# Three experts' items of at most 64 tokens, with high and low parts side by side

## The chip, the cores and the metric

One core of one Trainium2 chip runs the whole program. The metric is the device time of one execution in microseconds, from runs of the kernel before and the changed one. Engine names: TensorE (PE in rows, PEld its weight loads), VectorE (DVE), ScalarE (ACT), GpSimd (POOL), SyncE (SP), which issues most of the DMAs.

## What is computed

Two layers of a hybrid mixer on 256 tokens of 1024 values in float32. Layer 0 ends in a dense feed-forward stage, layer 1 in a mixture of experts, which is what the change is about:

```python
D_MODEL, N_EXPERTS, TOP_K, D_FF_EXPERT = 1024, 8, 2, 3584
logits = (ht @ w_router) + b_router
top_v, top_i = lax.top_k(logits, TOP_K)
probs = jax.nn.softmax(top_v, axis=-1)
gates = jnp.sum(jax.nn.one_hot(top_i, N_EXPERTS) * probs[..., None], axis=1)
for e in range(N_EXPERTS):
    a = jax.nn.silu(ht @ w_gate[e]) * (ht @ w_up[e])
    out = out + gates[:, e:e + 1] * (a @ w_down[e])
```

The 256 tokens make 512 choices of an expert. From the reference and its inputs, experts 0 to 7 get 54, 82, 58, 66, 52, 72, 42 and 86 of them.

## The kernel before

Every product is made of split operands: a float32 value is written as a high part (`whi`, `hhi`, `ahi`, rounded to `F32R`) and a low part, the rest. `mm3` (lines 763 to 766) then does three matmuls: high by high, low by high, high by low. In the expert stage the weights are the moving operand of 512 columns and the tokens, up to 128, the stationary one.

The expert stage works in items. An item is up to `CAP` = 128 tokens of one expert; items 0 to 7 are the experts in the order 0 to 7, and an expert with more than 128 tokens gets another item behind them (up to `ITEMS` = 11). Item 0 is written out by hand, items 1 to `last` - 1 run in a loop whose bound is a register read from `eid`, the last is written out again. An item has `E_CHUNKS` = 7 chunks of 512 hidden columns. A chunk takes six weight loads of 1 MB, slots s: two for gate, two for up, two for down.

The way of a slot: SP (`load`, line 477, called by `load_round`) fetches it into one of six ring places in `z` once VectorE has finished with the slot six before it. ScalarE writes its high part into a lane of `whi` (`e_hi_of`, line 418) once TensorE has used the lane's former slot, VectorE writes the low part (`e_lo_of`, line 424), and TensorE uses both. There are three or four lanes by the table `E_LANES`. The order on each engine is written by hand in `e_round`, `item` and `edge`:

- TensorE: `e_gate` into bank 0, `e_turn` of the former chunk's activations (four turns, line 773), `e_up` into bank 1, two `e_down` into banks 3 and 4, 24 matmuls each for gate, up and down. Near an item's end `turn_gathered` turns the next item's tokens.
- ScalarE: per chunk six casts of weights, the high part of the activations (`e_hi`, line 1628) and silu (line 1624). At an edge also the high part of the next tokens (`gathered_hi`, line 1617) and the item's output into `ysb` (`y_out`).
- VectorE: per chunk six subtractions of weights, the product silu by up (`e_mult`, line 2266) and the activations' low part (`e_lo`, line 1735). At an edge the low part of the next tokens (`e_lo_tokens`, line 1736).
- GpSimd: per item it gathers the next item's tokens from `tok_rows` by indirect DMA (line 736) and stores the item's rows to `out_rows` (line 738). At the end it gathers from `out_rows` the rows that each token needs, and VectorE adds them up with the gates' weights.

Routing: VectorE finds the two experts of each token, the places within each expert (`posx`) and, from the counts, `big`, `rank` and the table `eid` of each item's expert (lines 2244 to 2260), and sets `route_ok`. SP waits for it ahead of item 1's loads, and the other engines ahead of item 1. GpSimd waits for it too, works out each choice's row (lines 687 to 708), makes the late picks (line 711) that TensorE turns in item 0 (`turn_picks`), and writes and reads a table of tokens by item (lines 720 and 722).

## Time and profile before

| what | value |
|---|---|
| runs | 1728.37, 1728.77, 1729.31 us, median 1728.77 |
| profiled execution, span from its first to its last instruction | 1726.9 us |
| TensorE, VectorE, ScalarE, GpSimd busy | 1718.0, 1382.8, 1102.2, 111.9 us |
| bytes moved by DMA | 498.41 MB |

For the profiled execution the profile gives the span alone; what lies around the span is 1.9 us by the runs' median. Busy times are unions of an engine's instructions. Matmuls are pipelined, so one of 0.39 us starts every 0.23 us in a stream. A DMA share is the mean busy share of 16 DMA engines, and goes a little over 1 in short stretches. The expert stage begins at about 772 us and ends with the program.

### The profile page before, as it was taken

The numbers are of one execution on the slowest core, as the hardware profiler recorded it, in microseconds if no ns is written. First come the engines' busy times: TensorE is split into PE (matmuls) and PEld (weight loads), VectorE is DVE, ScalarE is ACT, GpSimd is POOL, SyncE is SP. The second block draws the span as 40 slices with busy tenths as digits, with TensorE's granted clock in tenths as the row PEclk, the third lists the DMA queues.
The fourth block names the chain that finished last, engine by engine and source line by source line (L and its number), as shares of the span: only waits on it lengthen the run. The fifth ranks groups of instructions, "written<-read, shape, count | busy, mean of one in ns | idle before, by whom it ended". The sixth has DMA issues, their size and how long they took to land.

```text
span 1726.9 us, 22649 instructions
## 1 busy us (share of the span) xinstructions
PE 1718.0 (99%) x8320; PEld 1435.9 (83%) x8320; DVE 1382.8 (80%) x1154; ACT 1102.2 (64%) x980; POOL 111.9 (6%) x114
## 2 busy tenths in 40 slices
PE   9999999999999999999999999999999999999998
PEld 8888888888888888888888888888888888888887
DVE  7875588555578755889889889889888898898898
ACT  4446564444344466557777777777777777777775
POOL 0021000000000200017000000000000000000100
PEclk9999999999999999999999999999999999999999
DMA  8653366553455424659999999999999999999994
GB/s 293 233 205 117 122 229 234 195 189 127 171 171 200 171 86 147 219 220 338 411 362 412 373 370 409 369 367 399 344 411 385 353 411 372 367 411 365 376 413 198
DMA packets 219848, 498.41 MB, mean 289 GB/s; under 512 B 8296, under 2 KB 13168, under 8 KB 219632
## 3 DMA queue, kind: packets, MB, share of 16 engines
q1 hardware_dynamic: 216096, 483.44, 75.6%
q0 software_dynamic: 3696, 14.18, 2.2%
q8 instruction: 40, 0.66, 0.1%
q14 instruction: 16, 0.13, 0.0%
HBM read 491.80 MB, written 7.88 MB: 289 GB/s over the span
## 4 chain that ended last, share of the span: by engine, by line
PE 96%; ACT 1%; DVE 1%; DMA 0%; issue 0%; POOL 0%; SPq 0%; DVEq 0%; POOLq 0%
PE ps L764 30%; PE ps L766 30%; PE ps L765 30%; PE ps L773 4%; PE ps L769 3%; ACT sb_w L1448 0%; DVE sb_wlo L395 0%; DMA sb_ringa<-in_w_in_dram 0%; ACT sb_whi L380 0%; DVE sb_w L1722 0%; ACT sb_ahi L1505 0%; DVE sb_z L1832 0%; ACT L1448 0%; DVE sb_wlo L424 0%; ACT sb_z L1498 0%
## 5 line engine op out<-in xcount | busy, mean ns | idle before, releaser
L424 DVE TENSOR_TENSOR sb_wlo<-sb_z,sb_whi 128x2048 fp32r<-128x2048 f32 x334 | 756.4, 2289 | 95.5 <-ACT sb_whi L418 94.8
L418 ACT ACTIVATE sb_whi<-sb_z 128x2048 fp32r<-128x2048 f32 x333 | 634.7, 1927 | 168.8 <-PE ps L766 164.9
L764 PE MATMUL ps<-sb_whi,sb_hhi 128*128 128x512 f32 (+2 forms) x1752 | 684.1, 390 | 0.0
L766 PE MATMUL ps<-sb_wlo,sb_hhi 128*128 128x512 f32 (+2 forms) x1752 | 676.0, 386 | 0.0
L765 PE MATMUL ps<-sb_whi,sb_hlo 128*128 128x512 f32 (+2 forms) x1752 | 675.7, 386 | 0.0
L766 PEld LDWEIGHTS ps<-sb_wlo,sb_hhi 128*128 128x128 f32 x1752 | 329.0, 188 | 66.8
L764 PEld LDWEIGHTS ps<-sb_whi,sb_hhi 128*128 128x128 f32 x1752 | 329.3, 188 | 65.3 <-issue 2.2
L765 PEld LDWEIGHTS ps<-sb_whi,sb_hlo 128*128 128x128 f32 x1752 | 329.4, 188 | 63.1
L764 PE MATMUL ps<-sb_whi,sb_ahi 128*128 128x512 f32 x560 | 219.1, 391 | 0.0
L766 PE MATMUL ps<-sb_wlo,sb_ahi 128*128 128x512 f32 x560 | 218.0, 389 | 0.0
L765 PE MATMUL ps<-sb_whi,sb_alo 128*128 128x512 f32 x560 | 218.0, 389 | 0.0
L395 DVE TENSOR_TENSOR sb_wlo<-sb_z,sb_whi 128x2048 fp32r<-128x2048 f32 (+1 forms) x70 | 153.3, 2197 | 75.0 <-ACT sb_whi L380 74.9
L380 ACT ACTIVATE sb_whi<-sb_z 128x2048 fp32r<-128x2048 f32 (+1 forms) x71 | 131.2, 1850 | 119.6 <-PE ps L766 118.5
L380 ACT ACTIVATE sb_whi<-sb_ringa 128x2048 fp32r<-128x2048 f32 x52 | 99.7, 1917 | 88.7 <-PE ps L766 76.8
L395 DVE TENSOR_TENSOR sb_wlo<-sb_ringa,sb_whi 128x2048 fp32r<-128x2048 f32 x52 | 118.6, 2286 | 31.2 <-ACT sb_whi L380 31.1
L766 PEld LDWEIGHTS ps<-sb_wlo,sb_ahi 128*128 128x128 f32 x560 | 105.1, 188 | 22.0
L765 PEld LDWEIGHTS ps<-sb_whi,sb_alo 128*128 128x128 f32 x560 | 105.2, 188 | 21.4
L764 PEld LDWEIGHTS ps<-sb_whi,sb_ahi 128*128 128x128 f32 x560 | 105.2, 188 | 21.4
L1628 ACT ACTIVATE sb_ahi<-ps 128x512 fp32r<-128x512 f32 x56 | 33.7, 602 | 42.7 <-PE ps L773 42.7
L773 PE MATMUL ps<-sb_const,sb_z 128*128 128x128 f32 x422 | 59.0, 272 | 0.5 <-DVE sb_z L2266 0.5
L773 PEld LDWEIGHTS ps<-sb_const,sb_z 128*128 128x128 f32 x422 | 50.5, 140 | 10.6 <-DVE sb_z L2266 0.9
L1735 DVE TENSOR_TENSOR sb_alo<-ps,sb_ahi 128x512 fp32r<-128x512 f32 x66 | 44.8, 685 | 14.6 <-ACT sb_ahi L1573 10.5
(274 smaller groups left out, 966.0 us busy)
## 6 DMA issues: line engine op xcount, KB each, us to landing
sb_z<-in_moe_w_gate_dram SPq DMA_DIRECT2D x112, 1024.0 KB, 6.9
sb_z<-in_moe_w_up_dram SPq DMA_DIRECT2D x112, 1024.0 KB, 6.8
sb_z<-in_moe_w_down_dram SPq DMA_DIRECT2D x112, 1024.0 KB, 7.1
sb_ringa<-in_w_in_dram SPq DMA_DIRECT2D x43, 1024.0 KB, 5.0
sb_z<-in_w_in_dram SPq DMA_DIRECT2D x24, 1024.0 KB, 5.0
sb_z<-in_ffn_w_up_dram SPq DMA_DIRECT2D x10, 1024.0 KB, 12.5
sb_z<-in_ffn_w_gate_dram SPq DMA_DIRECT2D x10, 1024.0 KB, 5.1
sb_z<-in_ffn_w_down_dram SPq DMA_DIRECT2D x10, 1024.0 KB, 5.0
```

What stands on the lines that cost most here:

```text
L380: nc.scalar.activation(whi[:, k, 0:n], raw[:, 0:n], ACT.Copy).then_inc(hi_done, 1)
L395: nc.vector.tensor_tensor(wlo[:, k, 0:n], raw[:, 0:n], whi[:, k, 0:n].bitcast(F32), ALU.subtract).then_inc(split, 1)
L418: nc.scalar.activation(e_lane(s)[0], ringb[:, s % RING_B, :], ACT.Copy).then_inc(hi_done, 1)
L424: nc.vector.tensor_tensor(lo, ringb[:, s % RING_B, :], hi.bitcast(F32), ALU.subtract).then_inc(split, 1)
L764: nc.tensor.matmul(out, lh, rh, start=start, stop=False)
L765: nc.tensor.matmul(out, ll, rh, start=False, stop=False)
L766: return nc.tensor.matmul(out, lh, rl, start=False, stop=stop)
L769: return nc.tensor.matmul(out, l, r, start=start, stop=stop)
L773: return nc.tensor.transpose(out, src, ident[0:n, 0:n])
L1628: nc.scalar.activation(ahi[:, :, at:at + CAP], ps[:, 2, :].rearrange("p (k c) -> p k c", k=4), ACT.Copy).then_inc(a_hi, 1)
L1735: return V.tensor_tensor(out, src, hi.bitcast(F32), ALU.subtract)
```

## The change

The seven experts 1 to 7 are ordered by their count of tokens (`fewer`, `order`), and that is the order of items 1 to 7. The first `FEW` = 3 of them hold up to `HC` = 64 tokens, the others 128; more tokens go to further items behind. In a small item the 64 tokens' high and low parts stand side by side as stationary columns (`hhi` holds high, high, low, high). Up and down take two matmuls instead of three, (high, low) by the weights' high part and by their low part, so that rows 0 to 63 and 64 to 127 of the result hold two summands. Gate must be whole in both halves, since silu comes next, and keeps three (`twice`). The turn multiplies by a constant of 64 columns that adds the halves, the activations then get their high and low part side by side in `ahi`, and for down the halves are added by the stores: GpSimd stores all 128 rows, waits, and stores rows 64 to 127 onto the first 64 with an adding DMA (`store_sum`). VectorE keeps four small operations of the routing; the rest goes to GpSimd, and `route_ok` is set by it after the table's stores. SP's program stays as it is.

```diff
+FEW = 3
+HC = P // 2
...
+            pool.wait_ge(rank_ok, 1)
+            link(pool.tensor_scalar(runs[:, 1:], order, FEW - 0.5, None, ALU.is_gt))
+            pool.tensor_scalar(room[:, 1:], runs[:, 1:], float(CAP - HC), float(HC), ALU.mult, ALU.add)
+            link(pool.tensor_scalar(first_of[:, 1:], order, 1.0, None, ALU.add))
+            link(pool.tensor_tensor(big, cnt, room, ALU.subtract))
+            link(pool.tensor_scalar(big, big, 0.5, None, ALU.is_gt))
+            link(pool.tensor_tensor(sums[:, 1, NE:], big, sums[:, 0, NE - 1:2 * NE - 1], ALU.add))
+            link(pool.tensor_tensor(sums[:, 2, NE:], sums[:, 1, NE:], sums[:, 1, NE - 2:2 * NE - 2], ALU.add))
+            link(pool.tensor_tensor(rank, sums[:, 2, NE:], sums[:, 2, NE - 4:2 * NE - 4], ALU.add))
+            link(pool.tensor_scalar(rank, rank, float(NE - 1), None, ALU.add))
+            pool.tensor_tensor(pos, posx, per_token(room), ALU.subtract)
+            link(pool.tensor_tensor(selx, rank, first_of, ALU.subtract))
+            link(pool.tensor_scalar(pos, pos, -0.5, None, ALU.is_gt))
             link(pool.tensor_tensor(item_, pos, per_token(selx), ALU.mult))
...
+            link(pool.tensor_scalar(more_of, rank, 1.0, None, ALU.add))
+            link(pool.tensor_tensor(more_of, more_of, big, ALU.mult))
+            link(pool.tensor_scalar(more_of, more_of, 1.0, None, ALU.subtract))
+            link(pool.tensor_tensor(found, places_of.unsqueeze(1).to_broadcast([P, ITEMS, 2 * NE]),
+                                    iota[:, 0:ITEMS].unsqueeze(2).to_broadcast([P, ITEMS, 2 * NE]), ALU.subtract))
+            link(pool.tensor_scalar(found, found, 0.0, None, ALU.is_equal))
+            for c in range(2):
+                m = pool.tensor_tensor(found[:, :, c * NE:(c + 1) * NE], found[:, :, c * NE:(c + 1) * NE],
+                                       iota[:, 0:NE].unsqueeze(1).to_broadcast([P, ITEMS, NE]), ALU.mult)
+            link(m)
+            for n in (8, 4, 2):
+                link(pool.tensor_tensor(found[:, :, 0:n], found[:, :, 0:n], found[:, :, n:2 * n], ALU.add))
+            pool.tensor_copy(eidf[:, 14:15], rank[:, NE - 1:NE])
+            pool.tensor_scalar(eidf[:, 15:16], rank[:, NE - 1:NE], 1.0, None, ALU.add)
+            link(pool.tensor_tensor(eidf[:, 0:ITEMS].unsqueeze(2), found[:, :, 0:1], found[:, :, 1:2], ALU.add))
+            pool.tensor_copy(eid[:, :], eidf[0:1, :]).then_inc(route_ok, 1)
...
+            def fetch_next(j):
+
                 wait_then(gather_mm, j * 2 + 2)
                 pool.tensor_copy(idx_now, idx[:, bass.ds(j + 13, 1)]).then_inc(idx_ok, 1)
                 wait_then(idx_ok, j + 1)
                 pool.indirect_dma_start(tok, None, tok_rows, at_rows(idx_now)).then_inc(tok_in, 16)
                 wait_then(y_ok, j + 1)
+
+            def store(j):
+
+                fetch_next(j)
                 pool.dma_start(out_rows[bass.ds(j * P, P), :], ysb[:, :]).then_inc(rows_out, 16)
+
+            def store_sum(j, n):
+
+                fetch_next(j)
+                pool.dma_start(out_rows[bass.ds(j * P, P), :], ysb[:, :]).then_inc(rows_half, 16)
+                wait_then(rows_half, n * 16 + 16)
+                pool.dma_start(out_rows[bass.ds(j * P, HC), :], ysb[HC:P, :], accum_op=ALU.add).then_inc(rows_out, 16)
+
+            store(0)
+            with pool.Fori(0, FEW) as n:
+                store_sum(n + 1, n)
+            with pool.Fori(FEW + 1, last) as j:
+                store(j)
...
+                def twice(out, k, hi, lo, start, stop):
+
+                    mm(out, hhi[:, k, HC:HC + P], hi, start, False)
+                    mm(out, hhi[:, k, 2 * HC:2 * HC + P], hi, False, False)
+                    return mm(out, hhi[:, k, 0:P], lo, False, stop)
+
+                def pair_of(out, parts, hi, lo, start, stop):
+
+                    mm(out, parts, hi, start, False)
+                    return mm(out, parts, lo, False, stop)
...
+                            if not few:
+                                m = mm3(ps[:, bank, :], hhi[:, k, 0:CAP], hlo[:, k, 0:CAP], hi[:, kk, :], lo[:, kk, :],
+                                        k == 0, k == KD - 1)
+                            elif bank == 0:
+                                m = twice(ps[:, bank, :], k, hi[:, kk, :], lo[:, kk, :], k == 0, k == KD - 1)
+                            else:
+                                m = pair_of(ps[:, bank, :], hhi[:, k, HC:HC + P], hi[:, kk, :], lo[:, kk, :],
+                                            k == 0, k == KD - 1)
...
                     for k in range(4):
-                        m = turn(ps[:, 2, k * P:(k + 1) * P], act_sb[:, 0, k * P:(k + 1) * P])
+                        if few:
+                            m = mm(ps[:, 2, k * HC:(k + 1) * HC], act_sb[:, 0, k * P:(k + 1) * P], halves)
+                        else:
+                            m = turn(ps[:, 2, k * P:(k + 1) * P], act_sb[:, 0, k * P:(k + 1) * P])
                     m.then_inc(a_t, 1)
...
+                            if few:
+                                m = pair_of(ps[:, 3 + half, :], ahi[:, k, at:at + P], hi[:, kk, cols], lo[:, kk, cols],
+                                            first and k == 0, last and k == 3)
+                            else:
+                                m = mm3(ps[:, 3 + half, :], ahi[:, k, at:at + CAP], alo[:, k, at:at + CAP],
+                                        hi[:, kk, cols], lo[:, kk, cols], first and k == 0, last and k == 3)
...
-                with pe.Fori(1, last) as j:
+                with pe.Fori(1, FEW + 1) as j:
+                    item(j, few=True)
+                with pe.Fori(FEW + 1, last) as j:
                     item(j)
...
+                        src, dst = gathered(n, k), hhi[:, k, 0:CAP]
+                        if few:
+                            src = src[:, 0:HC].unsqueeze(1).to_broadcast([P, 4, HC])
+                            dst = hhi[:, k, :].rearrange("p (c n) -> p c n", n=HC)
+                        m = nc.scalar.activation(dst, src, ACT.Copy, scale=par("norm2", KD + k))
...
-                def e_hi(n, at=0):
+                def e_hi(n, at=0, few=False):
                     act.wait_ge(a_t, n + (F_TILES + 1))
-                    nc.scalar.activation(ahi[:, :, at:at + CAP], ps[:, 2, :].rearrange("p (k c) -> p k c", k=4),
+                    c = HC if few else CAP
+                    nc.scalar.activation(ahi[:, :, at:at + c], ps[:, 2, 0:4 * c].rearrange("p (k c) -> p k c", k=4),
                                          ACT.Copy).then_inc(a_hi, 1)
...
-                link(V.tensor_scalar(big, ps[:, 4, 0:NE], float(CAP), None, ALU.is_gt))
-                link(V.tensor_tensor_scan(rank, ones[:, 0:NE], big, 0.0, ALU.mult, ALU.add))
-                V.tensor_scalar(eidf[:, 14:15], rank[:, NE - 1:NE], float(NE - 1), None, ALU.add)
-                link(V.tensor_scalar(eidf[:, 15:16], rank[:, NE - 1:NE], float(NE), None, ALU.add))
-
...
-                for n in range(EXTRA):
-                    second(n)
-                    pick_sum(iota[:, 0:NE], eidf[:, NE + n:NE + n + 1])
-                V.tensor_copy(eid[:, :], eidf[0:1, :]).then_inc(route_ok, 1)
+                link(V.tensor_copy(cnt, ps[:, 4, 0:NE]))
+                link(V.scalar_tensor_tensor(out=key, in0=cnt, scalar=float(NE), in1=iota[:, 0:NE], op0=ALU.mult,
+                                            op1=ALU.add))
+                others = [P, NE - 1, NE - 1]
+                link(V.tensor_tensor(fewer, key[:, 1:].unsqueeze(1).to_broadcast(others),
+                                     key[:, 1:].unsqueeze(2).to_broadcast(others), ALU.is_lt))
+                V.tensor_reduce(order, fewer, AX, ALU.add).then_inc(rank_ok, 1)
...
+                    c = HC if few else CAP
+                    lo = ahi[:, :, at + HC:at + P] if few else alo[:, :, at:at + CAP]
+                    minus_hi(lo, ps[:, 2, 0:4 * c].rearrange("p (k c) -> p k c", k=4), None,
+                             ahi[:, :, at:at + c]).then_inc(a_lo, 1)
...
+                        c = HC if few else CAP
+                        lo = hhi[:, k, 2 * HC:3 * HC] if few else hlo[:, k, 0:CAP]
+                        m = minus_hi(lo, gathered(j, k)[:, 0:c], par("norm2", KD + k), hhi[:, k, 0:c])
...
-                with dve.Fori(1, last) as j:
-                    edge(j - 1)
+                edge(0, few_next=True)
+                with dve.Fori(1, FEW) as j:
+                    item(j, few=True)
+                    edge(j, few=True, few_next=True)
+                item(FEW, few=True)
+                edge(FEW, few=True)
+                with dve.Fori(FEW + 1, last) as j:
                     item(j)
-                edge(last - 1)
```

On TensorE, in the loop over an item's chunks, the second half of a gate product, the turn and the following products stood so (`sb_whi`, `sb_wlo` are the weights' parts, `sb_hhi`, `sb_hlo` the tokens', `sb_ahi`, `sb_alo` the activations'; `sb_const` in the turn is the identity):

```order
L764 MATMUL ps<-sb_whi,sb_hhi 128x512
L765 MATMUL ps<-sb_whi,sb_hlo 128x512
L766 MATMUL ps<-sb_wlo,sb_hhi 128x512
...
L773 MATMUL ps<-sb_const,sb_z 128x128 x4
L355 REGISTER_ALU
L764 MATMUL ps<-sb_whi,sb_hhi 128x512
L765 MATMUL ps<-sb_whi,sb_hlo 128x512
L766 MATMUL ps<-sb_wlo,sb_hhi 128x512
...
L764 MATMUL ps<-sb_whi,sb_ahi 128x512
L765 MATMUL ps<-sb_whi,sb_alo 128x512
L766 MATMUL ps<-sb_wlo,sb_ahi 128x512
```

In a small item's loop the same place now reads:

```order
L833 MATMUL ps<-sb_whi,sb_hhi 128x512 x2
L833 MATMUL ps<-sb_wlo,sb_hhi 128x512
...
L833 MATMUL ps<-sb_const,sb_z 128x64 x4
L370 REGISTER_ALU
L833 MATMUL ps<-sb_whi,sb_hhi 128x512
L833 MATMUL ps<-sb_wlo,sb_hhi 128x512
...
L833 MATMUL ps<-sb_whi,sb_ahi 128x512
L833 MATMUL ps<-sb_wlo,sb_ahi 128x512
```

Gate keeps three matmuls for each of its eight parts, up and down have two; the turn is four matmuls with 64 columns.

On GpSimd, from the wait for the routing to the last operation before a choice's row is picked out, stood (the names in square brackets are semaphores; `pool_chain` is the engine's wait for its own former result):

```order
L687 TENSOR_SCALAR sb_st<-sb_st 128x8 [waits route_ok]
L688 TENSOR_TENSOR sb_st<-sb_st,sb_const 128x8 [waits pool_chain]
L689 TENSOR_SCALAR sb_root<-sb_st 128x16 [waits pool_chain]
L690 TENSOR_TENSOR sb_st<-sb_root,sb_st 128x16 [waits pool_chain]
L691 TENSOR_TENSOR sb_st<-sb_st,sb_const 128x16 [waits pool_chain]
L692 TENSOR_SCALAR sb_root<-sb_root 128x16 [waits pool_chain]
L693 TENSOR_TENSOR sb_root<-sb_root,sb_st 128x16 [waits pool_chain]
L694 TENSOR_SCALAR sb_st<-sb_st 128x16 [waits pool_chain]
L695 TENSOR_TENSOR sb_st<-sb_st,sb_root 128x16 [waits pool_chain]
L696 TENSOR_SCALAR sb_root<-sb_root 128x16 [waits pool_chain]
L697 TENSOR_TENSOR sb_st<-sb_root,sb_st 128x16 [waits pool_chain]
```

Now the same stretch begins with

```order
L705 TENSOR_SCALAR sb_const<-sb_const 128x7 [waits rank_ok]
L706 TENSOR_SCALAR sb_const<-sb_const 128x7 [waits pool_chain]
L707 TENSOR_SCALAR sb_const<-sb_const 128x7
L708 TENSOR_TENSOR sb_const<-sb_st,sb_const 128x8 [waits pool_chain]
L709 TENSOR_SCALAR sb_const<-sb_const 128x8 [waits pool_chain]
L710 TENSOR_TENSOR sb_const<-sb_const 128x8 [waits pool_chain]
L711 TENSOR_TENSOR sb_const<-sb_const 128x8 [waits pool_chain]
L712 TENSOR_TENSOR sb_st<-sb_const 128x8 [waits pool_chain]
L713 TENSOR_SCALAR sb_st<-sb_st 128x8 [waits pool_chain]
L714 TENSOR_TENSOR sb_root<-sb_st,sb_const 128x16 [waits pool_chain]
L715 TENSOR_TENSOR sb_st<-sb_st,sb_const 128x8
L716 TENSOR_SCALAR sb_root<-sb_root 128x16 [waits pool_chain]
```

and eight more follow as before, 20 operations instead of 11, and it waits for `rank_ok` instead of `route_ok`. Behind the table's four stores and ahead of its reading stands a block of 14 operations that was not there:

```order
L752 TENSOR_TENSOR sb_const<-sb_const 128x176 [waits pool_chain]
L754 TENSOR_SCALAR sb_const<-sb_const 128x176 [waits pool_chain]
L756 TENSOR_TENSOR sb_const<-sb_const 128x11x8 [waits pool_chain]
...
L761 COPY sb_st<-sb_st 128x1 [waits pool_chain]
L762 TENSOR_SCALAR sb_st<-sb_st 128x1
L763 TENSOR_TENSOR sb_st<-sb_const 128x11
L764 CAST sb_eid<-sb_st 1x16 [waits pool_chain]
L767 DMA sb_idx<-table_dram 128x11 [waits table_out]
L772 TENSOR_LOAD sb_eid [waits rows_filled,route_ok,tok_stored,table_rows]
```

Its last one sets `route_ok`, for which SP, TensorE, ScalarE and VectorE wait before item 1.

## Rows read from the trace of the kernel before

**Rows 1.** The page's busy times: engine, busy us, share of the span, instructions.

```profile
PE 1718.0 (99%) x8320; PEld 1435.9 (83%) x8320; DVE 1382.8 (80%) x1154; ACT 1102.2 (64%) x980; POOL 111.9 (6%) x114
```

**Rows 2.** Timeline, GpSimd: start us, us, line, operation, count, idle before.

```profile
1011.92 0.57 POOL L738 DMA_DIRECT2D out_rows_dram<-sb_ysb  x1 [114.18 <-ACT sb_ysb L1635]
...
1130.35 0.57 POOL L738 DMA_DIRECT2D out_rows_dram<-sb_ysb  x1 [114.19 <-ACT sb_ysb L1635]
```

**Rows 3.** Windows, one period: PE, PEld, DVE, ACT, POOL busy, clock, DMA share, GB/s.

```profile
892.90:1011.30 118.40, 118.40 (x542) 98.19 (x541) 104.98 (x65) 89.54 (x66) 3.38 (x3) 1.00 1.01 381
```

**Rows 4.** Timeline, TensorE, a chunk of an item in the loop.

```profile
1093.36 0.60 PE L773 MATMUL ps<-sb_const,sb_z 128*128 128x128 f32 x4
...
1099.27 0.39 PE L764 MATMUL ps<-sb_whi,sb_ahi 128*128 128x512 f32 x1
...
1104.71 0.39 PE L764 MATMUL ps<-sb_whi,sb_hhi 128*128 128x512 f32 x1
...
1110.15 0.60 PE L773 MATMUL ps<-sb_const,sb_z 128*128 128x128 f32 x4
```

**Rows 5.** Waits from 900 to 1700 us: us in total, times, longest.

```profile
ACT sb_whi L418 <- PE ps L766: 142.9, 169, 3.5
DVE sb_wlo L424 <- ACT sb_whi L418: 82.3, 132, 1.6
...
ACT sb_whi L418 <- DMA sb_z<-in_moe_w_up_dram: 1.8, 3, 0.7
```

**Rows 6.** Timeline, VectorE, the same chunk and the edge behind it.

```profile
1096.91 4.49 DVE L424 TENSOR_TENSOR sb_wlo<-sb_z,sb_whi 128x2048 fp32r<-128x2048 f32 x2 [1.24 <-ACT sb_whi L418]
1101.33 0.68 DVE L2266 TENSOR_TENSOR sb_z<-sb_z,ps 128x512 f32<-128x512 f32 x1
1101.92 4.52 DVE L424 TENSOR_TENSOR sb_wlo<-sb_z,sb_whi 128x2048 fp32r<-128x2048 f32 x2
...
1119.18 2.15 DVE L1736 SCALAR_TENSOR_TENSOR sb_hlo<-ps,sb_small,sb_hhi 128x128 fp32r<-128x128 f32 x8
```

**Rows 7.** Timeline, ScalarE, the same chunk.

```profile
1094.96 3.73 ACT L418 ACTIVATE sb_whi<-sb_z 128x2048 fp32r<-128x2048 f32 x2
```

**Rows 8.** Windows, an item's edge, columns as in group 3.

```profile
1120.00:1125.00 5.00, 5.00 (x25) 4.15 (x24) 4.61 (x9) 5.00 (x4) 0.00 (x0) 1.00 0.71 270
```

**Rows 9.** DMA from 1140 to 1200 us, then 1620 to 1700: bytes, issues, us to landing.

```profile
DMA packets 10516, 24.67 MB, mean 411 GB/s; under 512 B 399, under 2 KB 399, under 8 KB 10516
...
sb_z<-in_moe_w_gate_dram SPq DMA_DIRECT2D x6, 1024.0 KB, 6.7
...
DMA packets 13366, 33.04 MB, mean 413 GB/s; under 512 B 526, under 2 KB 526, under 8 KB 13364
...
sb_z<-in_moe_w_gate_dram SPq DMA_DIRECT2D x8, 1024.0 KB, 10.2
```

**Rows 10.** Timeline, GpSimd, the routing.

```profile
770.94 0.27 POOL L687 TENSOR_SCALAR sb_st<-sb_st 128x8 f32<-128x8 f32 x1 [5.84 <-DVE sb_eid L2260]
...
774.18 2.24 POOL L697 TENSOR_TENSOR sb_st<-sb_root,sb_st 128x16 f32<-128x16 f32 x1
...
803.20 2.71 POOL L720 DMA_INDIRECT table_dram<-sb_idx  x1 [0.61 <-issue]
...
829.64 2.20 POOL L736 DMA_INDIRECT sb_w<-tok_rows_dram,sb_idx  x1 [0.84 <-POOL sb_idx L734]
```

**Rows 11.** Timeline, TensorE in item 0: turn of the picks, of item 1's tokens.

```profile
817.19 0.38 PE L773 MATMUL ps<-sb_const,sb_z 128*128 128x128 f32 x2
...
873.73 1.04 PE L773 MATMUL ps<-sb_const,sb_w 128*128 128x128 f32 x8
```

**Rows 12.** Timeline, SyncE's queue, item 1's first loads.

```profile
869.83 3.09 SPq L477 DMA_DIRECT2D sb_z<-in_moe_w_gate_dram  x2
```

**Rows 13.** DMA from 900 to 1700 us, the token gathers.

```profile
sb_w<-tok_rows_dram,sb_idx POOLq DMA_INDIRECT x5, 9.2
```

**Rows 14.** Windows, the start of the program, columns as in group 3.

```profile
5.00:10.00 5.00, 3.39 (x31) 3.20 (x29) 2.34 (x5) 3.12 (x7) 0.00 (x0) 1.00 0.97 327
```

More of the change, by code:

```diff
@@ L246, in build, with ranked @@
         tok = w1t[:, 0, :]
+        at_rank = CONST["mlmask"][0]
+        def ranked(at, n):
+            return const[:, at_rank + at:at_rank + at + n]
+        places_of = ranked(0, 2 * NE)
+        room, runs, key = ranked(16, NE), ranked(24, NE), ranked(32, NE)
+        fewer = ranked(40, (NE - 1) * (NE - 1)).rearrange("p (a b) -> p a b", b=NE - 1)
+        order = ranked(92, NE - 1)
+        sums = ranked(100, 3 * 2 * NE).rearrange("p (s n) -> p s n", n=2 * NE)
+        found = ranked(148, ITEMS * 2 * NE).rearrange("p (i n) -> p i n", n=2 * NE)
+        halves = const[:, at_rank - HC:at_rank]
         ml_value = z[:, :, Z_MV:Z_MO].rearrange("p t (h n) -> p t h n", n=MDV + 1)
@@ L302, in build @@
             sem(n) for n in ("router_mm", "logit_sb", "x_quarter", "gather_pair"))
[L303 to L304 removed]
+        lg_mm, lg_e, lg_d, sel_ok, cnt_mm, rank_ok, route_ok = (
+            sem(n) for n in ("lg_mm", "lg_e", "lg_d", "sel_ok", "cnt_mm", "rank_ok", "route_ok"))
         pick_ok, gather_mm, gt_hi, gt_lo, y_ok = (
@@ L1206, in _, with e_product @@
                 fill(5)
-                def e_product(s, r, bank, item=None):
+                def twice(out, k, hi, lo, start, stop):
[5 more added lines that the diff above has]
+                    return mm(out, parts, lo, False, stop)
+                def e_product(s, r, bank, item=None, few=False):
                     for h in range(2):
@@ L1321, in item @@
                         e_round(E_HEAD + ROUND, n0 + 3, n0)
-                    with pe.Fori(1 if isinstance(j, int) else 0, (E_CHUNKS - 3) // 2) as i:
+                    with pe.Fori(1 if first_item(j) else 0, (E_CHUNKS - 3) // 2) as i:
                         for c in range(2):
@@ L1663, in item @@
                         nc.scalar.activation(spread[:, :], ps[:, 7, 0:S], ACT.Copy).then_inc(spread_sb, 1)
-                    with act.Fori(1 if isinstance(j, int) else 0, (E_CHUNKS - 3) // 2) as i:
+                    with act.Fori(1 if first_item(j) else 0, (E_CHUNKS - 3) // 2) as i:
                         for c in range(2):
                             s = E_HEAD + c * ROUND
-                            e_round(s, i * 2 + n0 + 2 + c, i * 2 + n0)
+                            e_round(s, i * 2 + n0 + 2 + c, i * 2 + n0, few)
                             for k in range(6, 10):
@@ L2117, in route_constants @@
                     V.tensor_copy(idx[:, 2 * TT:3 * TT], tokf)
+                    V.memset(sums[:, :, :], 0.0)
+                    V.memset(places_of[:, 0:1], 0.0)
+                    V.memset(room[:, 0:1], float(CAP))
+                    V.tensor_tensor(halves, ident[:, 0:HC], ident[:, HC:P], ALU.add)
                 x_add(0)
@@ L2298, in e_round, with item @@
                     e_mult(s + 3, n, r)
-                def item(j, more=True):
+                def item(j, more=True, few=False):
                     n0 = j * E_CHUNKS
@@ L2337, in _ @@
                 last = dve.value_load(eid[0:1, 14:15], min_val=NE - 1, max_val=ITEMS - 1)
-                with dve.Fori(1, last) as j:
-                    edge(j - 1)
+                edge(0, few_next=True)
+                with dve.Fori(1, FEW) as j:
+                    item(j, few=True)
+                    edge(j, few=True, few_next=True)
+                item(FEW, few=True)
+                edge(FEW, few=True)
+                with dve.Fori(FEW + 1, last) as j:
                     item(j)
-                edge(last - 1)
+                    edge(j)
                 item(last, more=False)
```

128 lines of the change are left out of this document (56 added, 72 removed).

## The prediction

> **What bounds the kernel now.** I read the busy times first: TensorE 99% of the span [rows 1]. Busy says little of stages, so next comes one period of the expert stage. GpSimd stores a finished item's rows every 1130.35 - 1011.92 = 118.43 us [rows 2], and the stretch of one period has TensorE busy throughout, VectorE 105 us, ScalarE 90 us, the DMA engines at a share of 1.0 with 381 GB/s [rows 3]. A share of 1.0 at only 381 GB/s is no proof of a full DMA; that needs the stretches below.
>
> TensorE's row shows why 118.4. Between two groups of turns lie 16.79 us, one chunk; 24 matmuls start in 1104.71 - 1099.27 = 5.44 us, 0.2267 us each [rows 4]. A chunk's 72 are 16.32 us, the four turns 0.47 us. Seven chunks and the turning of the next tokens make the period. In 800 us ScalarE waits 142.9 on TensorE, VectorE 82.3 on ScalarE, and for loads of the up weights, the largest such entry, ScalarE waits 1.8 [rows 5]: in the end all wait for TensorE.
>
> What would bind next is the point of this case. **VectorE:** two casts take 1101.33 - 1096.91 = 4.42 us of its time, 2.2 each, and the product a slot of 0.6 before the next cast starts [rows 6]; a chunk is 6 x 2.2 + 2 x 0.6 = 14.4 us. **ScalarE:** two casts run in 3.73 us [rows 7], 1.9 each at most, about 12 us a chunk with the two short ones. **DMA:** at each item's edge the loads slacken (270 GB/s), as VectorE frees nothing while it splits the tokens [rows 8]. Then the ring of six refills: 411 GB/s over 60 us with a load landing in 6.7 us, and 413 GB/s over 80 us with one landing in 10.2 us [rows 9]. More loads in flight land later and bring no more bytes: 411 to 413 GB/s is a ceiling here, not the pace of the consumers, who take 6.29 MB in 16.79 us, 375 GB/s.
>
> **The change part by part.** The counts of tokens, worked out from the reference's inputs, are 54, 82, 58, 66, 52, 72, 42, 86 for experts 0 to 7. Experts 6, 4 and 2 are the three fewest of 1 to 7, all at most 64, none is over 128: still 8 items, of which 1, 2 and 3 are small.
>
> TensorE, small item: gate keeps 24 matmuls a chunk, up and down fall from 24 to 16 each, so 56 x 0.2267 + 0.47 = 13.2 us a chunk. With nothing else in the way that is 16 x 7 x 0.2267 = 25.4 us an item, 76 us in all. The turn by the 64-column constant has four matmuls as before; I take the same 0.47.
>
> VectorE, small item: the six casts stay, 13.2 us; the product stays, 0.6; the low part halves its columns, at least 0.3: 14.1 us a chunk, 99 an item. The edge adds eight token splits (2.15 us now [rows 6], fewer columns later: 1.6) and a wait for ScalarE, whose token writes double their columns. Estimate: 104 us. ScalarE is near 88.
>
> DMA, small item: one period moves 381 x 0.1184 = 45.1 MB [rows 3]: 42 loads of 1.049 MB, the token gather and the row store. The added store of 64 rows is 0.26 MB: 45.4 MB, and at 412 GB/s **110.1 us**. This is the longest of the four, so it sets the item: 118.4 - 110.1 = 8.3 us saved, 24.9 in three. Two thirds of what TensorE drops only turn into TensorE waiting.
>
> Two corrections. The small items start with the ring part full: the plateau [rows 9] moved 24.67 MB where the consumers took 60 / 16.79 x 6.29 = 22.5, so 2 to 3 MB are missing at an item's start and some 3 MB of the six are there, half of it in flight. Drawing that down gives 0 to 7 us; I take 4. Against it, pauses at the edges cost the DMA 0 to 3 us an item, when too few loads are in flight; with six free slots I take 2 in all. The full item that follows asks 375 of 412 GB/s, so an empty ring costs it nothing.
>
> The Trainium skill (DMA: Bandwidth & Descriptors, "Where 436 GB/s comes from") speaks against the change: for transfers from HBM to SBUF the HBM side binds, at about 358 GB/s for a core. By that figure an item's 45.4 MB would need 127 us (an estimate), and the sum would be 26 us to the slow side. The trace disagrees: 411 to 413 [rows 9], and even the period's mean of 381 is above that figure [rows 3].
>
> GpSimd: routing moves to it and VectorE has 4 small operations instead of 11. Nothing follows from those, since VectorE's next step waits for ScalarE's tokens anyway (0 to 1 us gained). GpSimd's chain gets 9 more operations before the table. A small one takes a slot of 0.3 us in the free part, and 2.2 us beside a VectorE cast; the 41 up to the table's first store took 803.20 - 770.94 = 32.3 us, 0.8 each [rows 10]. Nine more are 7 us at most. The picks, done before 803.2, are wanted by TensorE at 817.2 [rows 11]: covered. Then come 14 more (some of 176 columns) ahead of route_ok: 11 us, doubled for the width 22, partly under the table's own transfers. So the token gather slips from 829.6 to 848 to 859; it lands 9.2 us later [rows 13] and TensorE wants it at 873.7 [rows 11]. SP needs route_ok for item 1's first load at 869.8 [rows 12] and would have it near 835. Cost: nothing; without this cover, one us for each us late. In the three small items GpSimd waits for its first store before it adds the second half: 8 us plus some 10, behind which only the next gather is queued, needed 90 us later, and ScalarE's next output, a period later. The adding store has no row before; between 0 (only its bytes, counted) and another full store of 0.52 MB, 1.3 us an item, I take 0, since it is the smaller transfer.
>
> **Sum:** 24.9 + 4 - 2 = 27 us off the profiled span of 1726.9, that is 1700. The runs' median is 1.9 above that span, so **1702 us**. A difference of 0.2% (3.5 us) is what can be told from no change.
>
> **The rivals.**
>
> VectorE sets the pace: were the ceiling a little higher for an unbroken stream, or the ring's stock larger, the item falls to VectorE's 104 us, 3 x 14.4 = 43 us off: 1686. For it: slices of 415 exist. Against: 80 us of ready loads never passed 413 in the mean.
>
> The chain between engines sets the pace: VectorE idles 1.24 us in a chunk after its low part, since ScalarE comes to its next cast only after the turn, the high part and silu [rows 6]. All its waits for ScalarE are 82.3 x 118.4 / 800 = 12.2 us an item [rows 5]. If they all stayed, an item would be 104 + 12 = 116 us, 7 us off in three; if two thirds stayed, 112 us, 19 off. In the middle 13 off: 1716. Against: these waits trace back to TensorE, and once TensorE is quicker ScalarE runs ahead of VectorE.
>
> The clock falls: TensorE works 13.2 of 15.7 us a chunk, in bursts with waits between. If the granted clock went to its lower level of 1.2 GHz, a chunk's matmuls would take twice 0.2267 each, 25.9 us a chunk, 10 us over the 15.7 of the forecast. It decides from about 3 of the 21 chunks on: the 27 us are gone. All 21 would be 1702 + 214 = 1916 us; half of them 1809. The Trainium skill (TensorE: Matmul & The Clock Gate, "Why this matters for your kernels") warns that idle gaps between bursts bring that level. Against: with TensorE busy 3.39 us of 5 the granted clock stayed 1.00 [rows 14], and here it is busy over 80%.
>
> The loads give less once they come without a break and adding stores run among them: below 45.4 MB / 118.4 us = 383 GB/s in all nothing is gained, at 370 an item is 122.7 us, 13 us slower in three. The page's figure above would be its extreme. Against: 60 and 80 us without a break at 411 and 413 [rows 9]. That the change does not do what it says (more than 64 tokens in a small item, so a ninth item at 118 us) is excluded by the counts unless TensorE's sums pick otherwise.
>
> **How the numbers follow.** DMA ceiling, 20 to 34 us off: 0.60. VectorE pace, 35 to 50 off: 0.14. Chain, 4 to 19 off: 0.18. No change: 0.03. Slower: clock 0.03, loads and a ninth item 0.02. Faster 0.92, same 0.03, slower 0.05. The range goes from the VectorE case (1686) to the chain case (1716); the wider ends and the slower cases stay outside, about 0.2 or less.
>
> **What would show it.** Stores of items 1 to 3 about 110 us apart, the others 118.4; 410 GB/s or more through the small items, and ScalarE waiting for DMA there, not for TensorE; TensorE busy near 85% in them at full clock; route_ok well before 869. Wrong if ScalarE's waits stay on TensorE, if the GB/s stay under 400 with VectorE idle (chain), or if the stretch shows a granted clock under 1.

## The result, and the profile after

| | before | after |
|---|---|---|
| median of the runs, us | 1729.04 (4 runs) | **1703.98** (1703.40 to 1705.37, 4 runs) |
| ratio, 95% interval | | 0.9858 (0.9844 to 0.9872) |
| span of the profiled execution, us | 1726.9 | 1701.7 |

The forecast was 1702.0, the range 1686 to 1716. The page of the changed kernel, its busy times, its DMA totals and the chain that ended last by engine:

```profile
PE 1672.3 (98%) x8068; PEld 1381.6 (81%) x8068; DVE 1376.5 (81%) x1147; ACT 1100.5 (65%) x980; POOL 140.0 (8%) x140
...
DMA packets 220095, 499.27 MB, mean 293 GB/s; under 512 B 8344, under 2 KB 13216, under 8 KB 219872
...
PE 77%; DMA 11%; DVE 5%; ACT 4%; issue 2%; SPq 0%; POOL 0%; DVEq 0%; ACTq 0%; POOLq 0%
```

TensorE has lost 46 us of busy time against [rows 1], and the DMA is now 11% of the chain. Where the time came from stands in GpSimd's stores (timeline; items 0, 1, 2, 3 and 4):

```profile
894.07 0.58 POOL L789 DMA_DIRECT2D out_rows_dram<-sb_ysb  x1 [47.31 <-ACT sb_ysb L1730]
...
1003.16 0.57 POOL L794 DMA_DIRECT2D out_rows_dram<-sb_ysb  x1 [104.68 <-ACT sb_ysb L1730]
1010.08 0.93 POOL L796 DMA_DIRECT2D out_rows_dram<-sb_ysb  x1 [6.35 <-DMA out_rows_dram<-sb_ysb]
...
1115.11 0.59 POOL L794 DMA_DIRECT2D out_rows_dram<-sb_ysb  x1 [99.85 <-ACT sb_ysb L1730]
...
1222.75 0.59 POOL L794 DMA_DIRECT2D out_rows_dram<-sb_ysb  x1 [95.61 <-ACT sb_ysb L1730]
...
1341.32 0.60 POOL L789 DMA_DIRECT2D out_rows_dram<-sb_ysb  x1 [107.78 <-ACT sb_ysb L1730]
```

The small items take 109.1, 112.0 and 107.6 us, 328.7 in sum where three periods of [rows 2] are 355.3: 26.6 less. The next full item is back at 118.6. Ahead of the first store and behind the last small item 1.4 us are lost, so the span is 25.2 shorter. The three small items and the full one behind them as windows (columns as in group 3):

```profile
894.10:1003.20 109.10, 103.06 (x459) 80.37 (x458) 103.02 (x65) 88.89 (x66) 3.61 (x4) 0.98 1.04 407
1003.20:1115.10 111.90, 104.46 (x458) 81.47 (x457) 103.78 (x65) 89.03 (x66) 4.87 (x4) 0.97 1.04 410
1115.10:1222.80 107.70, 101.77 (x457) 78.83 (x456) 101.86 (x65) 87.98 (x66) 4.92 (x5) 1.00 1.04 410
1222.80:1341.30 118.50, 118.50 (x542) 98.25 (x541) 106.55 (x66) 90.02 (x66) 3.58 (x4) 1.00 1.02 396
```

Against [rows 3] the DMA moves 407 to 410 GB/s instead of 381, and in the small items (the first three rows) no engine is busy throughout. The waits from 893 to 1230 us:

```profile
PEld ps L833 <- DVE sb_wlo L439: 32.9, 60, 2.1
ACT sb_whi L433 <- DMA sb_z<-in_moe_w_up_dram: 20.3, 31, 1.1
...
ACT sb_whi L433 <- DMA sb_z<-in_moe_w_gate_dram: 18.3, 29, 1.9
ACT sb_whi L433 <- PE ps L833: 17.6, 21, 2.2
DVE sb_wlo L439 <- ACT sb_whi L433: 17.4, 54, 1.5
```

Follow the waits back: TensorE waits for VectorE's low part, that for ScalarE's high part, and ScalarE for the loads, 20.3 us for the up weights and 18.3 for the gate weights, where 800 us of the kernel before had 1.8 [rows 5] and 1.0. The DMA view from 900 to 1222 us shows the plateau without the dips that came before at each item's edge [rows 8]:

```profile
DMA packets 55109, 132.37 MB, mean 411 GB/s; under 512 B 2096, under 2 KB 2096, under 8 KB 55105
...
sb_z<-in_moe_w_gate_dram SPq DMA_DIRECT2D x42, 1024.0 KB, 10.6
```

### The profile page after: what moved, and what is told of

The parts are those of the page before. It is cut to its first block, busy times and chain, and to the rows that moved or that the text cites. A ratio compares the mean times of both kernels' runs of the same rounds, so it can differ in the third digit from the quotient of the medians.

```text
span 1701.7 us, 22099 instructions
## 1 busy us (share of the span) xinstructions
PE 1672.3 (98%) x8068; PEld 1381.6 (81%) x8068; DVE 1376.5 (81%) x1147; ACT 1100.5 (65%) x980; POOL 140.0 (8%) x140
## 4 chain that ended last, share of the span: by engine, by line
PE 77%; DMA 11%; DVE 5%; ACT 4%; issue 2%; SPq 0%; POOL 0%; DVEq 0%; ACTq 0%; POOLq 0%
PE ps L828 23%; PE ps L830 23%; PE ps L829 23%; DMA sb_z<-in_moe_w_gate_dram 9%; PE ps L833 5%; DVE sb_wlo L439 3%; PE ps L837 3%; ACT sb_whi L433 2%; DMA sb_z<-in_moe_w_down_dram 2%; ACT sb_w L1538 0%; DVE sb_wlo L410 0%; DMA sb_ringa<-in_w_in_dram 0%; ACT sb_hhi L1711 0%; ACT sb_whi L395 0%; DVE sb_w L1824 0%
## 5 line engine op out<-in xcount | busy, mean ns | idle before, releaser
L828 PE MATMUL ps<-sb_whi,sb_hhi 128*128 128x512 f32 (+2 forms) x1416 | 551.9, 390 | 0.1
L830 PE MATMUL ps<-sb_wlo,sb_hhi 128*128 128x512 f32 (+2 forms) x1416 | 545.0, 385 | 0.0
L829 PE MATMUL ps<-sb_whi,sb_hlo 128*128 128x512 f32 (+2 forms) x1416 | 544.9, 385 | 0.0
L830 PEld LDWEIGHTS ps<-sb_wlo,sb_hhi 128*128 128x128 f32 x1416 | 265.9, 188 | 53.5
L829 PEld LDWEIGHTS ps<-sb_whi,sb_hlo 128*128 128x128 f32 x1416 | 266.3, 188 | 50.4
L833 PE MATMUL ps<-sb_whi,sb_hhi 128*128 128x512 f32 x504 | 173.7, 399 | 6.4 <-DVE sb_wlo L439 6.4
L830 PE MATMUL ps<-sb_wlo,sb_ahi 128*128 128x512 f32 x392 | 152.6, 389 | 0.0
L829 PE MATMUL ps<-sb_whi,sb_alo 128*128 128x512 f32 x392 | 152.6, 389 | 0.0
L410 DVE TENSOR_TENSOR sb_wlo<-sb_ringa,sb_whi 128x2048 fp32r<-128x2048 f32 x52 | 118.6, 2287 | 31.2 <-ACT sb_whi L395 31.1
L833 PE MATMUL ps<-sb_wlo,sb_hhi 128*128 128x512 f32 x336 | 131.4, 391 | 0.0
L828 PEld LDWEIGHTS ps<-sb_whi,sb_ahi 128*128 128x128 f32 x392 | 73.6, 188 | 16.3 <-DVE sb_wlo L439 0.8
```

The costliest lines, as they stand in the source:

```text
L410: nc.vector.tensor_tensor(wlo[:, k, 0:n], raw[:, 0:n], whi[:, k, 0:n].bitcast(F32), ALU.subtract).then_inc(split, 1)
L828: nc.tensor.matmul(out, lh, rh, start=start, stop=False)
L829: nc.tensor.matmul(out, ll, rh, start=False, stop=False)
L830: return nc.tensor.matmul(out, lh, rl, start=False, stop=stop)
L833: return nc.tensor.matmul(out, l, r, start=start, stop=stop)
```

## The experiments

The kernel before ran beside each group, at 1728.45 to 1728.65 us. Times are medians; ratios are to it. "Apart" is the distance of the stores behind items 1, 2 and 3.

**Is it the loads? A quarter of the bytes (e1), and half of VectorE's low parts on top (e5).**

```diff
+                if few:
+                    dst, src = dst[:, 0:1, 0:C], src[:, 0:1, 0:C]
```

> The changed kernel, but in the three small items each weight load brings a quarter of its bytes (the rest of the slot keeps old values, so those items' results are not the reference's). If DMA sets the small items: DMA falls to about 12 MB an item, and the item falls to what comes next, VectorE's 103 to 105 us: stores of items 1 to 3 about 104 us apart, 1704 - 3 x 5.5 = about 1687 us. If VectorE, TensorE with its clock, or the chain of waits sets them: within 3 us of 1704.

1682.06 us (1681.52 to 1683.66), ratio 0.9734 (0.9718 to 0.9750): 22 us below the change. Windows of items 1 to 3:

```profile
893.87:997.46 103.59, 101.03 (x459) 80.90 (x458) 101.18 (x65) 87.53 (x66) 3.61 (x4) 0.98 0.40 117
997.46:1099.45 101.99, 99.40 (x458) 79.27 (x457) 99.99 (x65) 87.01 (x66) 4.97 (x5) 1.00 0.42 121
1099.45:1201.35 101.90, 99.19 (x456) 78.95 (x455) 100.97 (x64) 86.20 (x66) 4.45 (x5) 1.00 0.53 163
```

With the same instructions on the engines, and the same number of loads, the items fall from 109.6 to 102.5 us: the bytes of the loads set the change's pace. What limits them to 411 GB/s, the memory or the DMA engines, no run here tells. VectorE is now busy 100 of 102. That it, and not TensorE, is the bound there is what the second kernel tells, in which it writes half of each low part too:

```diff
+            n = SLOT // 2 if short[0] else SLOT
```

> The changed kernel with both: a quarter of the bytes of each load and half of VectorE's low parts in the three small items. The run with a quarter of the bytes alone gave 1682.1 us and items of 103.6, 102.0 and 101.9 us. If VectorE set those, the items fall to TensorE's time, 7 x 13.2 + 1 for the token turns and some 3 at the edge = 96 to 98 us: 1682 - 3 x 5 = about 1667 us. If the chain of waits between the engines set them, within 3 us of 1682.

1667.86 us, ratio 0.9648 (0.9632 to 0.9664). Windows of items 1 and 2:

```profile
893.70:992.50 98.80, 97.79 (x461) 81.26 (x461) 59.97 (x64) 86.96 (x66) 2.51 (x3) 1.00 0.41 121
992.50:1090.40 97.90, 96.89 (x457) 80.52 (x457) 59.94 (x64) 86.80 (x66) 4.72 (x4) 1.00 0.45 126
```

Now TensorE is busy 97 of 98. The order of the bounds in a small item is so: DMA 109.6, VectorE 102, TensorE 97.

**VectorE's work alone (e3).** The half low parts, with whole loads.

> The changed kernel, but in small items VectorE makes the low part of only half of each weight slot (the other half keeps old values): each cast takes 1.1 instead of 2.2 us, 46 us less VectorE work in an item. If DMA sets the small items: 0 to 3 us less than 1704. If VectorE sets them: the item falls to DMA's or TensorE's time and more than 10 us go, if TensorE's waits at the edge matter 3 to 9 us.

1701.72 us (1700.60 to 1702.98), ratio 0.9843: 2.3 less than the change, within what the intervals leave open, though VectorE is busy only 183 us of 328 and the DMA gives 410 GB/s as before. In the profiled executions the three items take 328.2 us instead of 328.7. VectorE and the chain behind it hold no more than that.

**Back to three matmuls for up (e2).**

```diff
-                                m = pair_of(ps[:, bank, :], hhi[:, k, HC:HC + P], hi[:, kk, :], lo[:, kk, :],
-                                            k == 0, k == KD - 1)
+                                mm(ps[:, bank, :], hhi[:, k, HC:HC + P], hi[:, kk, :], k == 0, False)
+                                mm(ps[:, bank, :], hhi[:, k, HC:HC + P], lo[:, kk, :], False, False)
+                                m = mm(ps[:, bank, :], hhi[:, k, HC:HC + P], lo[:, kk, :], False, k == KD - 1)
```

> The changed kernel, but in small items up takes three matmuls again (the low part of the weights is added twice): 8 matmuls of 0.227 us more in each of 21 chunks, 38 us of TensorE work. If DMA sets the small items: a chunk of 64 matmuls is 15.0 us of TensorE, under DMA's 15.7, so 0 to 5 us more, 1704 to 1709. If TensorE sets them: 1742. If the chain does, something between, about 1720.

1710.07 us (1709.81 to 1710.25), ratio 0.9893 (0.9877 to 0.9910): 6.1 over the change, just past the upper end. It adds 8 x 7 x 3 x 0.2267 = 38 us of TensorE work, and 32 of them vanish under the loads. What is left shows where the cover ends: TensorE is now busy in 110.6 us of an item of 112.3. Its second item:

```profile
1006.20:1118.50 112.30, 110.56 (x513) 90.64 (x512) 101.81 (x65) 88.91 (x66) 4.27 (x4) 1.00 1.04 404
```

**Back to three for up and down (e9), then with the old turn too (e12).** The down product is edited in the same way.

> The change as it is, but in the three small items the up and the down products take three matmuls each as in the kernel before (high by high, high by low, and the low half of the weights once more in place of the third), so TensorE has its 72 matmuls of 0.2267 us a chunk back. The output isn't the reference's. If the whole gain is TensorE's 16 matmuls a chunk, TensorE sets the small items again and their stores come 118.4 us apart: 1704.0 + 3 x (118.4 - 109.6) = 1730.5, within 1728 to 1733. If the rest of the change (the places worked out on GpSimd, the adding stores, the product ahead of the turn) costs or gives something, the time leaves the kernel before by just that: above 1733 if it costs over 2 us an edge, under 1727 if it gives.

1739.52 us (1739.07 to 1739.55), ratio 1.0063 (1.0046 to 1.0080): 9 above what was expected, and **slower than the kernel before**. So something in the change costs 11 us once TensorE sets the pace. It stands in TensorE's timeline, first a small item's chunk, then a full one's, each with the matmul behind the turn:

```profile
1126.41 1.00 PE L833 MATMUL ps<-sb_const,sb_z 128*128 128x64 f32 x8
1127.22 0.48 PE L833 MATMUL ps<-sb_whi,sb_ahi 128*128 128x512 f32 x1
...
1391.94 0.60 PE L837 MATMUL ps<-sb_const,sb_z 128*128 128x128 f32 x4
1392.29 0.48 PE L828 MATMUL ps<-sb_whi,sb_hhi 128*128 128x512 f32 x1
```

The turn by the constant is four matmuls in the program and eight records in the trace; it holds TensorE 0.81 us where the four true transposes hold it 0.35. Times 7 chunks that is 3.2 us an item, and the items take 121.9, 121.7 and 121.6 us, 3.2 to 3.5 over 118.4. The second kernel puts the four transposes back:

```diff
-                            m = mm(ps[:, 2, k * HC:(k + 1) * HC], act_sb[:, 0, k * P:(k + 1) * P], halves)
+                            m = turn(ps[:, 2, k * P:(k + 1) * P], act_sb[:, 0, k * P:(k + 1) * P])
```

> The kernel of e9 (72 matmuls a chunk), and the turn in the small items is the four plain turns of the kernel before in place of the four products with the constant of 64 columns, so the two halves of the activations aren't summed and the output isn't the reference's. In e9 a chunk's turn holds TensorE 0.81 us until the next matmul starts, in a full item 0.35: 0.46 x 7 = 3.2 us an item, 9.7 in three. If that is all that e9 lost, this kernel stands at 1739.5 - 9.7 = 1729.8, within 1729 to 1731, and items 1 to 3 at 118.4 us. If the loss lies in the waits at the edges or in the adding stores, it stays at 1739.

1729.88 us (1729.43 to 1730.71, 10 runs), ratio 1.0008 (0.9998 to 1.0017). Its timeline of GpSimd, items 1, 2 and 3:

```profile
1012.98 0.58 POOL L794 DMA_DIRECT2D out_rows_dram<-sb_ysb  x1 [114.47 <-ACT sb_ysb L1733]
...
1131.59 0.60 POOL L794 DMA_DIRECT2D out_rows_dram<-sb_ysb  x1 [104.63 <-ACT sb_ysb L1733]
...
1249.92 0.59 POOL L794 DMA_DIRECT2D out_rows_dram<-sb_ysb  x1 [104.52 <-ACT sb_ysb L1733]
```

118.6 and 118.3 us apart, and item 1, behind item 0's store at 894.10, took 118.9. This closes the account: the turn costs 9.6 us while TensorE is the bound, and everything else in the change (the counts ordered on GpSimd, the adding stores, the wider token writes) 1.3 us together by the medians, which the interval doesn't tell from nothing; 3 us would be its upper end.

**Without the adding store (e6).** One store of 128 rows, nothing added.

> The changed kernel without the adding stores of 64 rows (the halves of a small item's rows are not added). If the adding store costs only its bytes, 0.26 MB at 410 GB/s: 0.6 us an item, 2 us in all, 1702. If it weighs on the DMA like a full store of 0.52 MB or more: 4 us or more. If nothing of it shows: 1704.

1701.49 us (1700.91 to 1702.62), ratio 0.9845 (0.9828 to 0.9861): 2.5 less by the medians, which is less than the 0.2% that the prediction calls tellable. An adding store's bytes are 0.26 MB / 0.411 = 0.64 us, 1.9 in three, so the bytes alone would do. The three items take 109.4, 109.1 and 109.1 us, 1.1 less in sum than in the change; the bytes of the two adding stores that fall among them are 1.3 us. A price of the adding store beyond its bytes isn't shown. With that store single items differ more (112.0 and 107.6 in the change, around a mean of 109.6); what moves time between them is open.

**A busy TensorE at the edge (e4).** Twenty matmuls whose result nobody reads, before the last turn of a small item.

```diff
+                    if few:
+                        for _ in range(20):
+                            mm(ps[:, 7, 0:P], ident, ident)
                     e_turn(n, few)
```

It was made for this in the change: TensorE timeline at the end of item 1,

```profile
989.72 0.39 PE L833 MATMUL ps<-sb_wlo,sb_ahi 128*128 128x512 f32 x1
992.99 1.10 PE L833 MATMUL ps<-sb_const,sb_z 128*128 128x64 f32 x8 [2.89 <-DVE sb_z L2361]
993.90 0.64 PE L833 MATMUL ps<-sb_whi,sb_ahi 128*128 128x512 f32 x1
994.34 0.63 PE L833 MATMUL ps<-sb_wlo,sb_ahi 128*128 128x512 f32 x1
```

and windows there and at the next edge:

```profile
994.00:997.00 3.00, 3.00 (x9) 2.32 (x9) 2.45 (x5) 2.79 (x3) 0.00 (x0) 0.51 1.05 408
...
1105.00:1107.00 2.00, 2.00 (x7) 1.61 (x6) 1.16 (x2) 1.72 (x3) 0.00 (x0) 0.50 1.05 410
1107.00:1110.00 3.00, 3.00 (x9) 2.32 (x8) 3.00 (x2) 1.67 (x2) 0.00 (x0) 0.50 1.05 407
```

TensorE idles 2.9 us for VectorE's product, then the granted clock stands at 0.50, 1.2 GHz: the matmuls start 0.43 us apart instead of 0.2267, for some 3.5 us here and 7 at the next edge. At the third edge it idles 2.68 us and the clock stays at 1.00.

> The changed kernel, but at the end of each small item TensorE does 20 matmuls of constants (2.4 us, nobody reads them) ahead of the last turn, where it now stands idle for 2.7 to 2.9 us and where the granted clock then falls to 0.50. If the idle stretch brings the lower clock, the granted clock stays at 1.00 in all three edges. If DMA sets the small items, the time stays within 1.5 us of 1704 all the same; if the slow stretches of the clock cost end to end, 5 us go (7 and 3 us at half clock lose half of that).

1703.76 us (1703.52 to 1704.02), ratio 0.9856: no difference. The clock is 1.00 in the same stretches, and from 1205 to 1225 us around the third edge:

```profile
990.00:994.00 4.00, 4.00 (x37) 3.96 (x37) 3.96 (x8) 4.00 (x10) 0.00 (x0) 1.00 1.05 409
994.00:997.00 3.00, 3.00 (x22) 2.74 (x21) 1.69 (x6) 2.36 (x3) 0.00 (x0) 1.00 1.06 410
1100.00:1103.00 3.00, 3.00 (x25) 2.84 (x24) 2.93 (x3) 3.00 (x8) 0.00 (x0) 1.00 1.05 408
1103.00:1110.00 7.00, 7.00 (x47) 6.32 (x46) 5.42 (x12) 6.09 (x6) 0.00 (x0) 1.00 1.05 408
```

The slow stretches are real and cost nothing, since the DMA goes on at 407 to 410 GB/s through them and TensorE, which needs less time for an item than the loads, catches up. The twenty matmuls themselves took longer than the 2.4 us expected:

```profile
990.06 4.63 PE L833 MATMUL ps<-sb_const 128*128 128x128 f32 x40
994.53 1.00 PE L833 MATMUL ps<-sb_const,sb_z 128*128 128x64 f32 x8
```

They hold TensorE 4.47 us, 0.22 each, and the turn behind them starts 1.5 us later than in the change; that too lies under the loads.

**How many, and in what order? Two small items (e7), four (e10), small and full in turn (e8), and that with a shorter token gather (e11).** The first two set FEW to 2 and 4. The third puts the small items at 1, 3 and 5 (the place of expert r of the order becomes 2r + 1), with the loops unrolled to match; the last gathers 64 rows of tokens for them instead of 128.

> The changed kernel with FEW = 2: the item of 58 tokens is a full one again. If each small item in a row is worth the same 8.3 us: about 1712.5 us. If the first is worth more than the later ones, since it draws the ring down: the loss is under 7 us, 1709 to 1711. Item 1 should stay at 109 us, item 2 near 110, item 3 at 118.4.

1712.41 us (1711.83 to 1713.05), ratio 0.9908: the third small item is worth 8.4 us.

> FEW = 4: the expert with the fourth fewest tokens, 66 of them, is put in items of 64 places, so it needs two of them and a ninth item is spent. If an item is worth what its loads take at the DMA's 411 GB/s, items 4 and the ninth cost 110 us where one of 118.4 stood: 1704 - 8.4 + 110 = 1805.6, or 1814 where the ninth is a full one. If the loads of an expert read a second time came quicker than 411 GB/s, the ninth would cost TensorE's or VectorE's pace (about 102) and the time would be under 1800.

1814.38 us (1813.73 to 1815.35), ratio 1.0498 (1.0481 to 1.0516). The expert of 66 tokens is two over the 64 places, and the ninth item, a full one (1814 in what was expected), costs its 118.4 less the 8 that the fourth small one gives.

> The changed kernel with the small items as items 1, 3 and 5 and full ones between them, so that the ring refills ahead of each. If the stock of the ring is worth 4 us to the first small item, as the forecast's sum has it, each now draws it: items of 106 to 109 us, 4 to 8 us less in all, 1696 to 1700. If the ring is empty at each item's start anyway, since VectorE frees nothing at the edge, three items of 109: 0 to 2 us less, 1702 to 1704. If the full items behind suffer: more than 1704.

1702.04 us (1700.83 to 1703.45), ratio 0.9845 (the change's interval holds it). The small items are 109.2, 109.5 and 109.6 us, each behind a full one; in its timeline items 0, 1, 2 and 3:

```profile
893.40 0.58 POOL L794 DMA_DIRECT2D out_rows_dram<-sb_ysb  x1 [40.02 <-ACT sb_ysb L1733]
...
1002.64 0.57 POOL L799 DMA_DIRECT2D out_rows_dram<-sb_ysb  x1 [104.84 <-ACT sb_ysb L1733]
...
1121.72 0.59 POOL L794 DMA_DIRECT2D out_rows_dram<-sb_ysb  x1 [106.09 <-ACT sb_ysb L1733]
...
1231.24 0.58 POOL L799 DMA_DIRECT2D out_rows_dram<-sb_ysb  x1 [105.25 <-ACT sb_ysb L1733]
```

A ring that a full item had stocked with 4 us of loads would show three small items near 106. It doesn't. But some stock there is, as the bytes of the first three of these stretches show:

```profile
893.40:1002.60 109.20, 103.08 (x459) 80.31 (x458) 103.52 (x65) 88.14 (x66) 3.60 (x3) 0.98 1.04 407
1002.60:1121.70 119.10, 118.71 (x541) 98.12 (x540) 104.52 (x65) 90.53 (x66) 4.50 (x4) 1.00 1.01 388
1121.70:1231.20 109.50, 104.05 (x457) 81.67 (x456) 103.93 (x65) 88.03 (x66) 3.45 (x3) 0.97 1.04 407
```

GB/s times length gives 44.4 and 44.6 MB for two small items, and 46.2 for the full one between them, where a period of the kernel before moves 45.1 [rows 3] and the adding store brings 0.26 more into the full one's stretch. A small item starts with 0.5 to 0.7 MB of its loads ahead, 1.2 to 1.7 us at 411 GB/s, and the full one makes them good, at 119.1 us instead of 118.4.

> The order of the earlier run in turn (items 1, 3, 5 small) and, for these items, a token gather of 64 rows in place of 128: 0.26 MB less in each of three items. If the DMA's pace sets the small items, that is 0.26 MB / 411 GB/s = 0.64 us each: 1702.0 - 1.9 = 1700.1. If the gather lies beside the loads at no price, 1702.0 as without it.

1701.26 us (1700.67 to 1704.28), ratio 0.9846: 0.8 under e8 with overlapping runs, so unclear. Its 2.7 us or 0.16% under the change is no difference that this measurement can tell. What went clearly lower here took bytes of weights away (e1, e5).

## Why the prediction was right, and where not

**The mechanism.** "This is the longest of the four, so it sets the item: 118.4 - 110.1 = 8.3 us saved" held: 109.6 us an item in the mean, 411 GB/s, ScalarE waiting for loads, and e1 gains 22 us by bytes alone. The third small item is worth 8.4 (e7). "Two thirds of what TensorE drops only turn into TensorE waiting" held as well: e2 gives back 38 us of its work for 6. Among its signs, "TensorE busy near 85% in them at full clock" did not come: TensorE was busy 93 to 94%, at a mean clock of 0.98 and 0.97 in the first two. Of that, the turn's 3.2 us an item and the slow stretches are accounted for below; the rest was not broken down.

**The second bound.** VectorE was put at 104 us and is busy 102 to 104; by e1 it would set 102. The rival that it sets the pace already needed a higher ceiling, and the DMA stayed at 411. The chain rival (112 to 116 us an item) fell too: VectorE's waits for ScalarE shrank to 17.4 us in three items (12.2 an item had been the figure before), and half of the work in VectorE's casts taken away gave 2.3 us by the medians (e3).

**TensorE's turn was mis-sized.** "The turn by the 64-column constant has four matmuls as before; I take the same 0.47" is wrong: a chunk's turn costs 0.46 us more, 3.2 an item, 9.7 in three (e9 and e12). So TensorE's own saving is 76 - 10 = 66 us. It did not touch the result, because the DMA's cover over TensorE is 12 us an item; in the prediction it was costed at nothing without naming that cover. This was the largest error of a term, and only an experiment that took the cover away showed it.

**The ring's stock.** "Drawing that down gives 0 to 7 us; I take 4" is about right as a total and not as the reserve of a single item. By the windows after the change the three small items moved 134.4 MB, where three periods of 45.1 and the two adding stores among them are 135.8, and the full item behind moved 46.9 where 45.4 were due: 1.4 to 1.5 MB were ahead at the start and made good at the end, some 3.5 us at 411 GB/s (an estimate). A small item by itself draws 1.2 to 1.7 us (e8), and three such draws come to little more than that one total. With the stock and the edges the sum had 330.3 - 4 + 2 = 328.3 us for the three items; they took 328.7. The span missed 1700 by 1.7 us because 1.4 were lost outside these items, for which the sum had no term.

**The adding store** was taken at nothing beyond its bytes, and nothing beyond them is shown: without it 2.5 us go by the medians, 1.9 of them its bytes (e6).

**The clock.** The rival was given 0.03, on the ground that TensorE busy 3.39 us of 5 kept its clock [rows 14]. Mean busy time was the wrong row to argue from: the clock fell twice behind idle stretches of 2.7 and 2.9 us, and with these filled it did not fall (e4). The Trainium skill (TensorE: Matmul & The Clock Gate, "Why this matters for your kernels") warns of idle gaps between bursts; two of three edges agree, while the third, idle for nearly as long, does not show it. "A granted clock under 1" was also named as a sign that the forecast is wrong. It came, and the forecast held: the sign was too strict, since it didn't ask whether TensorE sets the pace. The forecast's price for it, twice the time for a chunk, was right for the matmuls (0.43 us against 0.2267) and too high for the kernel at the length that occurred, some 10 us, as the loads run on (e4).

**GpSimd.** route_ok was expected near 835 and the token gather at 848 to 859. The timeline of the routing:

```profile
770.02 0.28 POOL L705 TENSOR_SCALAR sb_const<-sb_const 128x7 f32<-128x7 f32 x1 [4.63 <-DVE sb_const L2355]
...
800.36 7.40 POOL L738 TENSOR_SCALAR sb_z<-sb_const,sb_st 128x128 f32<-128x128 f32 x2
...
810.91 2.58 POOL L747 DMA_INDIRECT table_dram<-sb_idx  x1 [0.61 <-issue]
...
836.73 0.19 POOL L764 CAST sb_eid<-sb_st 1x16 int32<-1x16 f32 x1
...
844.43 2.33 POOL L783 DMA_INDIRECT sb_w<-tok_rows_dram,sb_idx  x1 [0.84 <-POOL sb_idx L781]
```

The first table store comes 7.7 us later than in [rows 10] (7 forecast), the picks at 807.8 against the 817 at which they were wanted, route_ok at 836.9, the gather 14.8 later. SP's first load of item 1 is wanted at 869.8 [rows 12], so all of it is covered, as forecast. It is thin at one place: the picks had 9.4 us in hand, a dozen more operations at the 0.8 us that one takes here in the mean.

**The rule on the HBM side** (the Trainium skill, DMA: Bandwidth & Descriptors, "Where 436 GB/s comes from", some 358 GB/s for a core) would have made the change 26 us slower. 132 MB at 411 GB/s over 322 us speak against it for this kernel. The same section works the figure out as half of what one stack of memory gives, for each of its two cores. This program runs on one core, so it was taken beyond the case for which it is worked out; no run here has a second core at work.
